# Last head of an HGRN2 layer: nine subtractions moved from VectorE to GpSimd, and the output projection's pieces placed elsewhere between the steps of the recurrence

## The reference

```python
q, f, i, z = split(rms_norm(x) @ w_in, 4)          # per head: 128 columns each
# per head h, over chunks of tokens:
o = A(q, k, f) @ v + (q * decay) @ S ;  S = decay * S + k.T @ v
o = rms_norm(o, g_onorm)
y = (o * silu(z)) @ w_out                          # sums over all 8 heads
x = x + rms_norm(y, norm_post)
```

## Time and profile before

| | us |
|---|---|
| median of 3 runs | 1077.96 (1077.11 to 1078.79) |
| the profiled execution's own time | 1079.18 |
| its span in the trace | 1077.5 |
| PE busy | 1052.9 (98% of the span) |
| DVE busy | 724.4 (67%) |
| ACT busy | 384.8 (36%) |
| POOL busy | 38.6 (4%) |

### The profile page before, as it was taken

How to read it: one execution, slowest core, us unless ns; L and a number is a source line. 1 busy time by engine, 2 the same in 40 slices (tenths; PEclk the granted TensorE clock), 3 DMA queues, 4 the chain that set the end, 5 groups by cost and what they waited for, 6 DMA issues and landing times.

```text
span 1077.5 us, 20495 instructions
## 1 busy us (share of the span) xinstructions
PE 1052.9 (98%) x8043; PEld 987.8 (92%) x8043; DVE 724.4 (67%) x1294; ACT 384.8 (36%) x730; POOL 38.6 (4%) x53
## 2 busy tenths in 40 slices
PE   6999999999999999999999999999999999979997
PEld 5999999999999888789999999999999999967885
DVE  7798677677677645655658595775859577575146
ACT  7443333333334433443243242414233241533123
POOL 1000000000000000000101010010101010010000
PEclk9999999999999999999999999999999999989999
DMA  7102121121121352122212211211221121121143
GB/s 231 33 20 79 42 77 39 39 78 39 39 78 58 115 181 99 64 64 59 60 42 60 60 41 58 60 40 41 58 61 41 56 61 58 42 79 59 47 174 123
DMA packets 93317, 74.30 MB, mean 69 GB/s; under 512 B 2519, under 2 KB 85528, under 8 KB 93274
## 3 DMA queue, kind: packets, MB, share of 16 engines
q1 hardware_dynamic: 75482, 64.80, 19.2%
q10 hardware_dynamic: 17792, 8.91, 2.8%
HBM read 60.26 MB, written 13.44 MB: 68 GB/s over the span
## 4 chain that ended last, share of the span: by engine, by line
PE 89%; DVE 7%; DMA 2%; issue 1%; ACT 1%; SPq 0%; DVEq 0%; ACTq 0%
PE bank L565 34%; PE bank L613 23%; PE bank L712 17%; PE bank L585 2%; PE bank L786 2%; PE bank L859 1%; PE bank L866 1%; PE bank L780 1%; PE bank L868 1%; DMA wraw<-in_w_in 1%; PE bank L816 1%; DMA arena<-in_x_prompt 1%; PE bank L727 1%; PE bank L693 1%; PE bank L689 1%
## 5 line engine op out<-in xcount | busy, mean ns | idle before, releaser
L565 PE MATMUL bank<-reg_a,wsplit 128*128 128x352 f32 x2304 | 388.5, 326 | 0.6 <-ACT arena L1236 0.6
L565 PEld LDWEIGHTS bank<-reg_a,wsplit 128*128 128x128 f32 x2304 | 367.8, 188 | 4.0 <-issue 2.4
L613 PE MATMUL bank<-reg_a,wsplit 128*128 128x264 f32 x1344 | 165.5, 284 | 0.0
L613 PEld LDWEIGHTS bank<-reg_a,wsplit 128*128 128x128 f32 x1344 | 164.1, 188 | 0.0
L613 PE MATMUL bank<-reg_b,w_ring 128*128 128x264 f32 x1008 | 125.0, 284 | 1.0 <-ACT arena L1091 1.0
L613 PEld LDWEIGHTS bank<-reg_b,w_ring 128*128 128x128 f32 x1008 | 123.3, 188 | 1.3 <-DVE arena L1545 1.0
L712 PE MATMUL bank<-reg_a,reg_b 128*128 128x512 f32 x288 | 71.3, 402 | 0.9 <-DVE reg_a L1426 0.9
L712 PE MATMUL bank<-reg_b,reg_a 128*128 128x512 f32 x288 | 68.7, 395 | 0.0
L712 PEld LDWEIGHTS bank<-reg_a,reg_b 128*128 128x128 f32 x288 | 55.0, 192 | 14.3 <-DVE reg_a L1426 1.3
L712 PEld LDWEIGHTS bank<-reg_b,reg_a 128*128 128x128 f32 x288 | 53.9, 188 | 12.6
L1614 DVE TENSOR_TENSOR arena<-arena,bank 128x264 f32<-128x264 f32 x84 | 34.8, 427 | 33.6 <-PE bank L613 32.4
(11 more groups left out here) (260 smaller groups left out, 1481.9 us busy)
## 6 DMA issues: line engine op xcount, KB each, us to landing
wraw<-in_w_in SPq DMA_DIRECT2D x64, 512.0 KB, 4.0
arena<-in_x_prompt SPq DMA_DIRECT2D x16, 512.0 KB, 3.6
wraw<-in_w_out SPq DMA_DIRECT2D x16, 512.0 KB, 3.3
x_scratch<-arena SPq DMA_DIRECT2D x8, 512.0 KB, 2.6
arena<-in_state_hgrn ACTq DMA_DIRECT2D x8, 512.0 KB, 3.9
out<-arena ACTq DMA_DIRECT2D x8, 512.0 KB, 3.0
arena<-x_scratch SPq DMA_DIRECT2D x8, 512.0 KB, 3.2
out<-arena SPq DMA_DIRECT2D x7, 512.0 KB, 2.9
```

Source lines behind the costliest of these rows:

```text
L565: mm = nc.tensor.matmul(bank[b][:, 0:CH], w[wi][:, k, :], rhs[hi], start=(k == 0 and i == 0), stop=(k == KT - 1 and i == 2))
L613: mm = nc.tensor.matmul(bank[banks[q]][:, 0:QT], w[wi][:, k, :], B_OP[name][hi][:, k, q * QT:(q + 1) * QT], start=(start and k == 0 and i ...
```

## The change

Nine subtractions of the last head's stretch go from DVE to POOL: the low parts of the eight tiles of the output weights, and of head 6's outputs. They keep their events. POOL makes tile 0 before its three instructions for the last head, tiles 1 and 2 after them, then head 6's outputs, then tiles 3 to 7. On PE the fillers move one step forward, tile 5 goes ahead of level 64, and `keep_pace` is gone. ACT splits tile 2 one step sooner, and the tiles 3 to 6 and one of the last two likewise; it moves the parts 0 to 2 behind s=8, ahead of the last split, no longer waiting for all low parts (that wait now stands ahead of part 4). `o_part` gives `r_q` and `r_vr` to the token tiles 0 and 1 and `wraw` to 2 and 3. DVE waits for `o_lo` of head 6 ahead of the last gate.

```diff
-            rows = (wraw[:, 0].rearrange("p k c -> p (k c)"), wraw[:, 1].rearrange("p k c -> p (k c)"), r_q, r_vr)[i]
+            rows = (r_q, r_vr, wraw[:, 0].rearrange("p k c -> p (k c)"), wraw[:, 1].rearrange("p k c -> p (k c)"))[i]
...
-        SPLIT_OUT = {3: (1,), 4: (2,), 5: (3,), 6: (4,), 7: (5,), 8: (6, 7)}
+        SPLIT_OUT = {3: (1, 2), 4: (3,), 5: (4,), 6: (5,), 7: (6,), 8: (7,)}
...
-            for h in range(KT):
+            def out_lo(k):
+
+                hi, lo = [w.rearrange("p (k c) -> p k c", k=KT) for w in wout_tile(reg_a, k)]
+                pool.wait_ge(w_lo, NW3 + k)
+                pool.wait_ge(w_hi, NW3 + k + 1)
+                pool.tensor_tensor(lo, wraw[:, k % 2], hi.bitcast(F32), ALU.subtract).then_inc(w_lo, 1)
+
+            for h in range(KT - 1):
                 spread_v(h)
+            out_lo(0)
+            spread_v(KT - 1)
+            out_lo(1)
+            out_lo(2)
+            pool.wait_ge(o_hi, KT - 1)
+            at = (KT - 2) * 2 * T
+            pool.tensor_tensor(reg_b[:, at + T:at + 2 * T], r_o, reg_b[:, at:at + T].bitcast(F32), ALU.subtract).then_inc(o_lo, 1)
+            for k in range(3, KT):
+                out_lo(k)
...
-            FILL = {3: (0,), 4: (1,), 5: (2,), 6: (3,), 7: (4,), 8: (5, 6)}
+            FILL = {3: (0, 1), 4: (2,), 5: (3,), 6: (4,), 7: (6,)}
...
-            def keep_pace(b, n):
-
-                for k in range(n):
-                    nc.tensor.transpose(bank[b][:, 0:P], ident[:, :], ident[:, :])
...
-                if s == 4:
-                    pe.wait_ge(AR.sem, AR.at(KT - 1, "vt"))
-                    keep_pace(5, 8)
                 if s == 7:
                     rec(KT - 1, MID, KT - 2)
-                    pe.wait_ge(VR.sem, VR.at(KT - 1, "c16"))
-                    keep_pace(4, 8)
-                if s == 8:
-                    pe.wait_ge(VR.sem, VR.at(KT - 1, "c32"))
-                    keep_pace(3, 6)
+                    first_parts(5)
                 rec(KT - 1, s, KT - 2)
...
+                if s == 8:
+                    move_parts(0, 3)
                 for k in SPLIT_OUT.get(s, ()):
                     split_out(k)
-                if s == 9:
-                    act.wait_ge(w_lo, NW3 + KT)
-                    move_parts(0, 3)
                 if s == 10:
                     move_parts(3, 4)
+            act.wait_ge(w_lo, NW3 + KT)
             move_parts(4, 2 * PARTS)
...
-                if s == 1:
-                    split_lo(NW3 + 1, 0)
-                if s == 5:
-                    turn_lo(KT - 2)
-                for k in SPLIT_OUT.get(s, ()):
-                    hi, lo = [w.rearrange("p (k c) -> p k c", k=KT) for w in wout_tile(reg_a, k)]
-                    split_lo(NW3 + k + 1, k % 2, lo, hi)
+            dve.wait_ge(o_lo, KT - 1)
             gate(KT - 1)
```

## The result

The changed kernel takes 1085.61 us (median of 4 runs, 1084.39 to 1087.53) against 1077.53 us for the kernel before in the same session: a ratio of 1.0076, 95% interval 1.0059 to 1.0093, or 8.1 us slower. The forecast was 2.8 us slower, with a range that ended at 1084.6 us: the right side, the wrong size. The profiled execution is one of the longer ones (1086.70 us, span 1085.0, 7.5 us more than the span before).

A forecast was written before the change was run, and what follows sets the result against it. PE's chain of waits bounds the kernel, its end moving with u. u at 983.3 us plus 2.1 and 1.0 for half clock gave 986.4, 2.8 us later than before: 1080.8 us, range 1075.9 to 1084.6.

The forecast's parts named there:

- The bound: From the start of u PE is fully busy, so the kernel's end moves one to one with u.
- The port and the turns: GpSimd reads and VectorE instructions with two SBUF inputs block each other on one port, alternating one instruction each.
- it cancels: Rival: VectorE keeps the port through L1928 to L1940; 1077 to 1079.5 us; chance 0.24.
- The price of a subtraction: Each GpSimd subtraction priced at 1.90 us from L521, with 2.70 us as upper end.
- The rival of a slower GpSimd: GpSimd subtractions slower than 1.90 us: 1083.6 us at 2.3 each, 1086.4 at 2.70; chance 0.18.
- Tile 0: Its GpSimd subtraction delays the chain to the diagonal blocks by 0.8 us, leaving +0.15 us after L521.
- Nearly taken back: Tile 0's 0.8 us mostly recovered: L521 avoids VectorE's subtraction, so L1915 ends at 949.8, before 949.65.
- Tile 1: GpSimd makes it 949.8 to 951.7 us, so PE's idle of 4.36 us shrinks to some 1 us.
- Level 8 to snew: Level 8 starts at 960.2 us, level 16 at 964.2, and snew comes at 975.2, before 974.52.
- at one in two: Chance of a clock fall behind tile 2, costing level 8 0.7 and tile 3's products 1.3 us; 1.0 counted.
- Tile 6: PE idles 5.2 us before its products; u at 983.3 us at full clock, plus 2.1 us for half clock.
- The rival "faster": VectorE and GpSimd mostly run side by side; 2.2 to 3.4 us sooner, 1075.2 us; chance 0.16.

The follow-up runs named there:

- e3: The kernel before plus eight GpSimd subtractions in the last head's stretch whose results nobody reads; 1089.26 us, ratio 1.0106.
- e4: The kernel before plus eight GpSimd memsets that only write SBUF in the last head's stretch, and 15 later subtractions; 1078.56 us, ratio 1.0009.
- e6: The changed kernel with 16, 36 and 40 identity transposes ahead of the diagonal blocks, level 8's transpose and tile 6's products; 1083.33 us, ratio 1.0049.
- e1: The changed kernel with its nine subtractions back on VectorE, keeping the new filler order and no keep_pace; 1081.75 us, ratio 1.0037 to the kernel before.
- e8: The kernel before with only tile 0's subtraction on GpSimd, ahead of its three last-head instructions; 1077.14 us, ratio 0.9995.
- e10: The kernel before plus five forms of the subtraction, three times each, on GpSimd alone behind VectorE's last instruction; dense 2.34 us, no kernel time given.

## Why the prediction was right in kind and wrong in size

Taken by its own steps, with u forecast at 986.4 us and found at 991.02, 4.6 us later:

- **The bound.** Right: the end moved one to one with u (7.5 against 7.42 us), and PE is as busy behind u as before, so ACT's and `o_part`'s edits cost nothing there.
- **The port and the turns.** The port is right, and shown by e3 against e4. The turns are right in the main: neither engine keeps the port through its whole queue, which the case "it cancels" needed of VectorE. But they are not one instruction each: GpSimd had two in a row (L521 and the one at 949.10 us), VectorE two (L1935 and the L1932 at 957.36). "All of L1884 to L1936" have two SBUF inputs was too much: the two reciprocals among them have one, and L1907 and L1918 read a bank. The Trainium skill's rule (SBUF — State Buffer, "Who interferes with whom") holds in both its halves: reads block, a memset does not block two-input instructions.
- **The price of a subtraction.** This step failed: 1.90 us was taken from L521; the measured ones are 2.34 to 2.40 us unhindered. Its upper end of 2.70 us held. The rival of a slower GpSimd came nearest: 1083.6 us at 2.3 us each and 1086.4 at 2.70, against 1085.6 measured. At 2.35 us its own rule, seven times the difference, gives an estimated 1083.9: the price is the largest part, but not all. The Trainium skill's figure (GPSIMD Engine Reference, section 3.1), an estimated 2.25 us, was nearer than the row chosen.
- **Tile 0.** L1888 took 1.80 us for 0.43, and PE's wait ahead of the diagonal blocks grew by 1.3 us (2.50 for 1.18), where the forecast had 0.8: the price again. The absolute times below hide it, since this trace reaches the last head 0.76 us sooner. "Nearly taken back" behind L521 failed, because GpSimd kept the port there for tile 1.
- **Tile 1.** "GpSimd 949.8 to 951.7": it came at 951.47, since GpSimd took it directly behind L521 and ahead of the waiting L1919, two instructions in a row. PE's gain came as forecast, but L1919 ended at 951.75 instead of 949.8. The first L1932 got going at 953.9 (its end less 1.20 us), 2.3 us later than forecast, and behind it came two turns of GpSimd, 2.2 us each, for the three of 1.76 forecast: 953.9 + 3.2 + 4.4 = 961.5. k3c came at 961.46, for 960.0. With 1.90 us in the order that the trace has, k3c would come near 959.5 (an estimate: four GpSimd instructions at 0.5 us less each), so the price is enough to explain this step.
- **Level 8 to snew.** This is the second step that failed. Forecast 975.2, found 979.92: 1.5 us of the 4.7 were there at k3c, 3.2 came in this step. It took level 8 and tile 3's products at full clock and put 1.0 us aside for a fall "at one in two". The fall came and held from 958.90 to 969.14: level 8 took 1.92 us, tile 3's products 4.21, level 16 1.67, for 1.13, 2.35 and 1.12 us at full clock. It began after 2.48 us without work, not 3.46. From the start of level 8 to that of level 16 the forecast has 4.0 us, e6 at full clock 4.8, the changed kernel 6.0: at full clock the step is 0.8 us too short, since GpSimd holds VectorE for longer than forecast, and the clock adds 1.2. A third fall, at 948.66, 1.7 us after the idle of 2.50 us that tile 0's subtraction lengthened, stood in no term of the sum, and cost nothing: the products under it end at about 954.1, where tile 2's low part comes (954.01).
- **Tile 6.** The idle was forecast at 5.2 us and was 5.67; the fall behind it was forecast too. From snew to u the trace has 11.1 us, the forecast, with its 2.1 us of clock, 10.2. That the removed transposes "stood in idle time" and cost nothing is doubtful: with (many more) transposes in this idle e6 has no fall there and gets from snew to u in 8.5 us.
- **The rival "faster"** rested on engines side by side; e3 excludes it. What was not among the rivals is that the new order of PE's fillers, with `keep_pace` gone, costs 4.3 us even with VectorE doing the subtractions (e1): my sum had carried it inside the steps (tile 3's products ahead of level 16, tile 6's ahead of the transposes) and never set it apart.

By place the excess of 4.6 us is 1.5 us at k3c, 2.2 us between k3c and snew beyond the 1.0 put aside, and 0.9 us behind snew. By cause the parts are not independent, and how they divide exactly is open: in e6's trace 4.9 us less of half-clock loss give back 1.9 us.

## What to carry to other kernels

Before moving elementwise work from VectorE to GpSimd, look at what VectorE runs beside it. Here, next to instructions that read two SBUF tensors, each reading GpSimd instruction stood in VectorE's queue with its own, longer, time (2.34 us for 1.22), and a 16-column instruction took 2.4 us. One such subtraction away from the tight stretch (e8) cost nothing. Before an engine is changed, ask which single result the bound engine waits for; here one subtraction of 1.2 us, moved ahead of 3.2 us of other work on the same engine, gave 4.6 us, the clock's falls included. Price an instruction by a row with the same access pattern, not only the same size.

## What the runs showed of the hardware that was not expected

- A GpSimd `tensor_tensor` over 1024 columns takes 1.90 us when its second input repeats each element over 128 columns, and 2.34 us when both are dense; a repeated block in the first input and fewer partitions change nothing (e10).
- Who gets the port when both engines want it is not settled by who has waited longer. At 949.10 us GpSimd's next subtraction went ahead of a VectorE instruction that had stood since 948.32; at 953.97 and 957.37 VectorE went first, though GpSimd's waits were met there too. In e6, with the same instructions on both engines at that point, GpSimd went first at 957.41, and the second 1024-column scaling took 3.45 us where it had 1.21. In e3 L1925 was held for 4.21 us. What decides is open.

```profile
957.40 3.45 DVE L1945 TENSOR_TENSOR arena<-arena,r_tt 128x1024 f32<-128x1024 f32 x1
```

- In the changed kernel the clock fell 1.7 us behind an idle of 2.50 us (at 948.66) and 2.48 us into another (at 958.90), while in e8 an idle of 2.55 us in the first place brought no fall there, and in e6 the fall at 967.86 had, with the transposes counted as work, no idle longer than 1.36 us in the ten microseconds before it. The length of an idle alone does not tell. Half clock held for 2.9 to 10.2 us in the traces before and after, and for 13.6 us in e3, where PE idled 11.81 us. The four runs of the changed kernel have mean clocks of 0.993 (1084.4 and 1084.5 us) and 0.989 (1086.7 and 1087.5 us), so the time at half clock differs from run to run.
